# Turning the gated product of eight feed-forwards on VectorE instead of TensorE

## What is computed

```python
D_MODEL, SEQ, D_FF = 1024, 256, 2816

def swiglu(h, w13, w2):                    # feed-forwards 0 to 3
    a, b = jnp.split(h @ w13, 2, axis=-1)
    return (jax.nn.silu(a) * b) @ w2

def _half_ffn(x, g_pre, g_post, w_gate, w_up, w_down):   # feed-forwards 4 to 7
    h = _rmsnorm(x, g_pre)
    f = (jax.nn.silu(h @ w_gate) * (h @ w_up)) @ w_down
    return x + 0.5 * _rmsnorm(f, g_post)

mod = c_act @ ada_w[l] + ada_b[l]          # 9 x 1024 columns for each layer of the first block
sh1, sc1, g1, sh2, sc2, g2, sh3, sc3, g3 = jnp.split(mod, N_ADA, axis=-1)
```

## Time and profile before

| | |
|---|---|
| median of 3 runs | 2158.02 us (2157.7 to 2168.08) |
| span of the profiled execution | 2156.2 us |
| TensorE busy | 2100.3 us |
| VectorE busy | 1474.4 us |
| ScalarE busy | 1002.2 us |
| mean granted TensorE clock | 0.995 |
| transposes of the gated product (L793) | 352 matmuls |
| ScalarE's copy of it (L1615), 80 of them to g_hi | 577 ns |
| VectorE's low part of it (L2332), 80 of them to g_lo | 683 ns |

### The profile page before, as it was taken

How to read it: one execution, slowest core, us unless ns; L and a number is a source line. 1 busy time by engine, 2 the same in 40 slices (tenths; PEclk the granted TensorE clock), 3 DMA queues, 4 the chain that set the end, 5 groups by cost and what they waited for, 6 DMA issues and landing times.

```text
span 2156.2 us, 31249 instructions
## 1 busy us (share of the span) xinstructions
PE 2100.3 (97%) x12249; PEld 1832.9 (85%) x12249; DVE 1474.4 (68%) x2058; ACT 1002.2 (46%) x1415; POOL 31.1 (1%) x33
## 2 busy tenths in 40 slices
PE   7999999999999999999999999999999999989998
PEld 5888998888888988888888888888887888988887
DVE  7988878888888646674465558975457546677444
ACT  3434555334443555443364446464446445555443
POOL 0000000000000000000000000010000000001000
PEclk9999999999999999999999999999999999999999
DMA  8888446886787441275555542235554554425552
GB/s 343 302 309 306 164 174 227 318 307 239 295 298 264 152 142 46 74 275 191 177 168 182 194 176 104 73 102 211 184 186 164 187 190 143 155 79 178 193 181 92
DMA packets 75606, 417.46 MB, mean 194 GB/s; under 512 B 5888, under 2 KB 6016, under 8 KB 51840
## 3 DMA queue, kind: packets, MB, share of 16 engines
q1 hardware_dynamic: 75520, 416.27, 53.9%
HBM read 415.20 MB, written 1.05 MB: 193 GB/s over the span
## 4 chain that ended last, share of the span: by engine, by line
PE 88%; DVE 7%; ACT 2%; DMA 1%; issue 1%; SPq 0%; DVEq 0%; ACTq 0%
PE AB L750 13%; PE AB L752 13%; PE AB L751 13%; PE Y L293 9%; PE Y L295 9%; PE Y L294 9%; PE AB L293 2%; PE AB L295 2%; PE AB L294 2%; PE Y L1377 2%; DVE lo L2074 2%; PE N L793 2%; PE M L693 1%; PE Y L750 1%; PE Y L751 1%; PE Y L752 1%
## 5 line engine op out<-in xcount | busy, mean ns | idle before, releaser
L2074 DVE TENSOR_TENSOR lo<-raw,hi 128x2048 fp32r<-128x2048 f32 x310 | 708.3, 2287 | 384.3 <-ACT hi L1527 383.8
L1527 ACT ACTIVATE hi<-raw 128x2048 fp32r<-128x2048 f32 x322 | 615.0, 1913 | 539.5 <-PE Y L295 254.7
L750 PE MATMUL AB<-hi,h_hi 128*128 128x512 f32 x1280 | 506.4, 396 | 1.5 <-DVE lo L2074 1.5
L752 PE MATMUL AB<-hi,h_lo 128*128 128x512 f32 x1280 | 499.3, 390 | 0.0
L751 PE MATMUL AB<-lo,h_hi 128*128 128x512 f32 x1280 | 498.3, 389 | 0.0
L752 PEld LDWEIGHTS AB<-hi,h_lo 128*128 128x128 f32 x1280 | 240.3, 188 | 51.3
L750 PEld LDWEIGHTS AB<-hi,h_hi 128*128 128x128 f32 x1280 | 240.4, 188 | 49.2 <-DVE lo L2074 1.7
L751 PEld LDWEIGHTS AB<-lo,h_hi 128*128 128x128 f32 x1280 | 240.7, 188 | 47.9
L293 PE MATMUL Y<-g_hi,hi 128*128 128x256 f32 x664 | 188.2, 283 | 0.0
L294 PE MATMUL Y<-g_lo,hi 128*128 128x256 f32 x664 | 187.9, 283 | 0.0
L295 PE MATMUL Y<-g_hi,lo 128*128 128x256 f32 x664 | 187.8, 283 | 0.0
(11 more groups left out here) (437 smaller groups left out, 3223.2 us busy)
## 6 DMA issues: line engine op xcount, KB each, us to landing
raw<-slabs SPq DMA_DIRECT2D x322, 1024.0 KB, 5.0
ada_raw<-ada SPq DMA_DIRECT2D x34, 2048.0 KB, 8.1
ada_raw<-ada SPq DMA_DIRECT2D x2, 1024.0 KB, 14.8
kT<-ada SPq DMA_DIRECT2D x1, 1024.0 KB, 10.3
vt<-ada SPq DMA_DIRECT2D x1, 1024.0 KB, 12.3
x<-x_t SPq DMA_DIRECT2D x1, 1024.0 KB, 14.3
out_t<-x SPq DMA_DIRECT2D x4, 256.0 KB, 3.0
vec<-vectors SPq DMA_DIRECT2D x1, 462.0 KB, 3.1
```

Of the source, the lines that this page charges most:

```text
L750: nc.tensor.matmul(out_, h_hi[:, k, at], w_hi, start=start, stop=False)
L752: return nc.tensor.matmul(out_, h_lo[:, k, at], w_hi, start=False, stop=stop)
L1527: nc.scalar.activation(hi[slot][:, :], raw[slot][:, :], ACT.Copy).then_inc(hi_done[slot], 1)
L2074: nc.vector.tensor_tensor(lo[slot][:, :], raw[slot][:, :], hi[slot][:, :].bitcast(F32), ALU.subtract).then_inc(lo_done[slot], 1)
```

## The change

LAY_FROM is 0, so every condition `f < LAY_FROM` is false, and all eight feed-forwards change. In steps 1 to 10 TensorE no longer turns the gated product; at the end of steps 1 to 9 it only waits for `gf_done`. VectorE, between the split of the second up slab and the split of the down slab, runs `lay_gated`: sixteen block transposes, each of 32 partitions and 4 blocks of 32 columns, from `gf` into `silu`, with the signal `g_laid` on the last. ScalarE's `g_split` and VectorE's `gate_lo` read `silu` instead of N. Since `silu` now holds the turned product until `gate_lo` has read it, ScalarE's next silu waits for `glo_done` as well. The eleventh product of each feed-forward still goes through TensorE and N.

```diff
--- before.py
+++ after.py
@@ -253,6 +253,7 @@
         h_half = sem("h_half")
         acc_ready = sem("acc_ready")
         g_turned = sem("g_turned")
+        g_laid = sem("g_laid")
         ot_ready = sem("ot_ready")
         maps_ready = sem("maps_ready")
         head_var = sem("head_var")
@@ -463,6 +464,8 @@
             return [((j + r) % 3, (j + r) // 3 - 1) for r in range(3)]
 
         DEFERRED = (6, 8, 9, 10, 11)
+
+        LAY_FROM = 0
 
         def pre_gain(n):
             l, j = divmod(n - 6, 3)
@@ -901,7 +904,7 @@
                 def step(i, ada, first=False, last=False):
                     pe.wait_ge(lo_done[ring[0][0]], i + (ring[0][1] + 1))
                     up(ring[0][0], 0)
-                    if first:
+                    if first and f < LAY_FROM:
                         turn_gated(i + g0)
                     pe.wait_ge(lo_done[ring[1][0]], i + (ring[1][1] + 1))
                     up(ring[1][0], 1)
@@ -911,7 +914,10 @@
                     def behind():
                         if ada:
                             cols(i + (q0 - 1))
-                        turn_gated(i + (g0 + 1))
+                        if f < LAY_FROM or last:
+                            turn_gated(i + (g0 + 1))
+                        else:
+                            pe.wait_ge(gf_done, i + (g0 + 1))
 
                     down(ring[2][0], first=first, between=behind if last else None)
                     if not last:
@@ -1610,9 +1616,18 @@
                     else:
                         nc.scalar.activation(h_hi[:, k, :], hf[:, k, :], ACT.Copy).then_inc(hh_ready, 1)
 
-            def g_split(g, to=g_hi):
-                act.wait_ge(g_turned, g + 1)
-                nc.scalar.activation(to[:, :], N[:, :], ACT.Copy).then_inc(ghi_done, 1)
+            def g_split(g, f):
+
+                if f < LAY_FROM:
+                    act.wait_ge(g_turned, g + 1)
+                else:
+                    act.wait_ge(g_laid, g - (LAY_FROM * NSTEP + f - LAY_FROM) + 1)
+                nc.scalar.activation(g_hi[:, :], N[:, :] if f < LAY_FROM else silu[:, :], ACT.Copy).then_inc(ghi_done, 1)
+
+            def last_g_split(f):
+
+                act.wait_ge(g_turned, (f + 1) * NSTEP if f < LAY_FROM else LAY_FROM * NSTEP + f - LAY_FROM + 1)
+                nc.scalar.activation(z_hi[:, :], N[:, :], ACT.Copy).then_inc(ghi_done, 1)
 
             def ffn(f):
                 g0 = c.take("g", NSTEP)
@@ -1622,9 +1637,11 @@
                 j0 = c.take("slab", 3 * NSTEP - 4) - 1
                 (sa, na), (sb_, nb), (sw, nw) = step_slots(j0)
 
-                def silu_of(a, slot, n):
+                def silu_of(a, slot, n, g=None):
 
                     act.wait_ge(used[slot], n)
+                    if f >= LAY_FROM and g is not None:
+                        act.wait_ge(glo_done, g)
                     if f >= 4:
                         for t in range(TT):
                             ins = nc.scalar.activation(silu[:, t * T:(t + 1) * T], a[:, t], ACT.Silu,
@@ -1638,11 +1655,11 @@
                     if first and f >= 4:
                         split(sb_, i + nb)
                         act.wait_ge(root_ready, TT * c["stat"] + TT)
-                    silu_of(a_, slot_b, n_b)
+                    silu_of(a_, slot_b, n_b, None if first else i + (g0 - 1))
                     if not (first and f >= 4):
                         split(sb_, i + nb)
                     split(sw, i + nw)
-                    g_split(i + (g0 - 1))
+                    g_split(i + (g0 - 1), f)
                     if a:
                         split(sa, i + (na + 1))
 
@@ -1654,11 +1671,11 @@
                 step(NSTEP - 1, ab_tok[:, :, A], sb_, NSTEP - 1 + nb, a=False)
                 j = c["slab"] - 2
                 next_slab()
-                silu_of(ab_tok[:, :, A], j % 3, j // 3 + 1)
+                silu_of(ab_tok[:, :, A], j % 3, j // 3 + 1, g0 + NSTEP - 1)
                 n_ahead = min(2, NSLAB - c["slab"])
                 if n_ahead:
                     next_slab()
-                g_split(g0 + NSTEP - 1, z_hi)
+                last_g_split(f)
                 if f >= 4:
                     c.take("stat")
                 sqrt_table()
@@ -2327,9 +2344,19 @@
                                                          ALU.mult)
                 ins.then_inc(gf_done, 1)
 
-            def gate_lo(g, to_hi=g_hi, to_lo=g_lo):
+            def lay_gated(g):
+
+                dve.wait_ge(gf_done, g + 1)
+                src = gf[:, :].rearrange("p (t c n) -> p c t n", t=TT, c=2)
+                to = silu[:, :].rearrange("p (c t n) -> p c t n", c=2, t=TT)
+                for a in range(0, P, 32):
+                    for b in range(0, P, 32):
+                        ins = nc.vector.transpose(to[b:b + 32, :, :, a:a + 32], src[a:a + 32, :, :, b:b + 32])
+                ins.then_inc(g_laid, 1)
+
+            def gate_lo(g, src, to_hi=g_hi, to_lo=g_lo):
                 dve.wait_ge(ghi_done, g + 1)
-                nc.vector.tensor_tensor(to_lo[:, :], N[:, :], to_hi[:, :].bitcast(F32), ALU.subtract
+                nc.vector.tensor_tensor(to_lo[:, :], src[:, :], to_hi[:, :].bitcast(F32), ALU.subtract
                                         ).then_inc(glo_done, 1)
 
             def ffn(f):
@@ -2355,8 +2382,10 @@
                     gated(i + (g0 - 1), b)
                     if not (first and f >= 4):
                         split(sb_, i + nb)
+                    if f >= LAY_FROM:
+                        lay_gated(i + (g0 - 1))
                     split(sw, i + nw)
-                    gate_lo(i + (g0 - 1))
+                    gate_lo(i + (g0 - 1), N if f < LAY_FROM else silu)
                     if out_:
                         mod_out(i + (q0 - 2))
                     if mac_:
@@ -2374,7 +2403,7 @@
                 gated(g0 + NSTEP - 1, ab_tok[:, :, B])
                 if c["slab"] < NSLAB:
                     split(c["slab"] % 3, c["slab"] // 3)
-                gate_lo(g0 + NSTEP - 1, z_hi, z_lo)
+                gate_lo(g0 + NSTEP - 1, N, z_hi, z_lo)
                 if n_ada == NSTEP - 1:
                     c["last_mod"] = q0 + NSTEP - 2
                 if n_ada:
```

## The result

The changed kernel takes 2254.41 us (median of 4 runs, 2251.56 to 2255.12), the kernel before 2157.86 us beside it: ratio 1.0433, 95% interval 1.0416 to 1.045. That is 96.5 us slower. The span of the profiled execution is 2252.7 us against 2156.2, so its difference is 96.5 us as well.

The account below looks back on a forecast made before the run. TensorE bounds the kernel; VectorE would bound steps with modulation work. Feed-forwards 0 and 1 add 74.2 us, 2 adds 27.4, 3 adds 4.9, 4 to 7 give back 8.8: 97.7, plus 13.6 for the clock, 2269.3 us; range 2200 to 2310.

Parts of the forecast that it names:

- The bound moves to VectorE in loaded steps: In steps with modulation work, VectorE would need 20.65 us where TensorE needs 16.98, so TensorE waits for the gate product.
- loaded steps: The 30 of 80 steps that carry modulation work on VectorE, in feed-forwards 0 to 3; 17.34 us long before the change.
- The price of the block: VectorE's sixteen transposes per step: 0.31 us each plus 0.02 us between, 5.3 us together, called L.
- 34 places: Where the block's length was taken to be on the path: 20 + 8 + 2 + 4 over the feed-forwards.
- Priced as L2409 overlaps, 3.7 us: Rival: VectorE's transposes overlap as independent full-width operations do, block 3.7 us, kernel 2208 us; chance 0.17.
- pieces on different quarters run side by side: Rival: VectorE's sixteen transposes cost what four full-width ones do, 1.24 us, fitting into the idle; kernel 2122 us; chance 0.04.
- The law, 34 L - 82.5: Time added to the whole kernel in us, before the clock, for a VectorE block of L us; 97.7 us forecast.
- The crossing of 2.4 us a block: The VectorE block length per step at which gain and loss cancel, 0.15 us per piece.
- What the removal gives: Four TensorE transposes fewer per step, 0.45 us each group; at most 36 us over all 80.
- light steps: The 50 of 80 steps without modulation work; VectorE has room, and steps were to shrink from 16.81 to 16.36 us.
- The first step of feed-forwards 4 to 7: TensorE would wait 2.3 us for the low part, less 0.45 for the removed turn: +1.8 us each.
- The clock: TensorE's granted clock falls after its waits, costing 1.7 us once per feed-forward, 13.6 us in all.

Follow-up runs that it names:

- e6: The changed kernel with one in-place transpose of 128 partitions x 512 elements instead of sixteen, so the product is not the true one: 2129.28 us, ratio 0.9844.
- e4: The changed kernel with each of the sixteen transposes writing to the partitions it reads, so no block moves between quarters: 2201.34 us, ratio 1.0189.
- e5: The changed kernel with only the eight transposes that read the lower 64 partitions, half of the product left unturned: 2166.15 us, ratio 1.0037.
- e9: The changed kernel with the block's two loops swapped: the quarter written stays for four transposes, the quarter read changes at each; 2253.51 us, ratio 1.0449.
- e2: The changed kernel with only pieces 1 to 9 of feed-forwards 4 to 7 turned on VectorE, the rest on TensorE as before: 2141.22 us, ratio 0.9908.
- e1: The changed kernel with only feed-forwards 4 to 7 turning on VectorE, 0 to 3 as before the change: 2154.1 us, ratio 0.9962.
- e7: The changed kernel with TensorE's wait in loaded steps filled by zero matmuls into the free bank N, same results computed: 2252.28 us, ratio 1.0421.

## Why the prediction was right

I forecast 2269.3 us in a range of 2200 to 2310; it came to 2254.4. Of the 111.3 us, 96.5 came.

- **The bound moves to VectorE in loaded steps.** Right, by the full VectorE in feed-forward 0, by the step of 20.34 us (20.65 forecast), and by e6, where the same path with a short block is faster than before. Step less block is 15.27 us in the changed kernel and in e4, and 15.26 in e5: only the block changes VectorE's step.
- **The price of the block.** 5.3 us forecast, 5.07 measured: 0.303 us a transpose (0.31) and 0.014 us between (0.02). Times 34 places this is 7.8 us of the miss. Both halves of the estimate came from operations of another kind: the duration from a transposing reduction with its length scaled down, the distance from four additions of 4 elements that change quarters. Neither was luck. The step from 512 elements to 128 costs (705 - 303) / 384 = 1.05 ns an element between e6's transpose and these, as the subtraction assumed (1.044). And e4 and e9 show that the distance was right for its reason. Priced as L2409 overlaps, 3.7 us, the block would have been about e4's 3.60 us, and the forecast 46 us too low (2208 us). That pieces on different quarters run side by side is refuted: each starts after the one before has ended.
- **The law, 34 L - 82.5.** With the measured 5.07 us it gives 89.9 us, and the eight feed-forwards measured 91.8, of which 1.6 are the clock in feed-forward 6. It also carried e5 and e4 within 3 us. The crossing of 2.4 us a block fits e5: at 2.54 us the kernel is 0.4% slower than before. It doesn't reach down to e6 (0.71 us), where loaded steps are TensorE's again.
- **What the removal gives.** 0.45 us forecast, 0.48 measured in feed-forwards 4 to 7 (16.80 to 16.32) and 0.44 in 2 and 3 (17.10 to 16.66). The sum over light steps was therefore slightly low.
- **The first step of feed-forwards 4 to 7.** A wait of 2.3 us was forecast ahead of the down product. The timeline of TensorE, feed-forward 4 (answering):

```profile
1236.83 0.47 PE L294 MATMUL Y<-hi,g_hi 128*128 128x512 f32 x1 [2.24 <-DVE g_lo L2359]
```

  e2 removes it by leaving piece 0 on TensorE, and gains 2.0 us per feed-forward over e1.
- **The clock.** This is the term that was mis-sized: 13.6 us forecast, as one exposed fall of 3.4 us, worth 1.7, for each feed-forward. The falls came (mean clock 0.978), and inside loaded steps they are hidden, as e7 shows. Exposed were 6.0 us between feed-forwards 0 and 1 (3.9) and 1 and 2 (2.1), and one fall in feed-forward 6, about 1.6 us. At the ends of 0 and 1 the fall is there as forecast, but lasts 6.8 us; the rest of the 3.9 fits a further fall of 3.4 us in the mixer behind feed-forward 0, at 358.9. The kernel before and e7 have none there, but whether the edit brings it is not shown. Feed-forwards 2 and 3 took the path back without a visible fall, and in 4, 5 and 7 the wait of 2.2 us brought none. With the 1.5 us that the kernel before loses between 4 and 5 and the changed one doesn't, the clock made 6.1 instead of 13.6 us, which is 7.5 us of the miss.

TensorE's timeline where feed-forward 0 ends (answering), then slices of 2 us behind feed-forward 0, in the mixer, and behind feed-forward 1 (stretch, length, TensorE busy, clock, DMA share, GB/s):

```profile
255.04 0.49 PE L639 MATMUL M<-ada_lane,over_quads 128*128 128x128 f32 x2 [3.17 <-DVE ada_lane L2134]
257.93 1.11 PE L796 MATMUL N<-ident,gf 128*128 128x128 f32 x4 [2.40 <-DVE gf L2336]
...
258.00:260.00 2.00, 2.00 (x10) 0.50 0.83 250
260.00:262.00 2.00, 2.00 (x11) 0.50 0.98 414
...
360.00:362.00 2.00, 2.00 (x12) 0.50 0.00 0
...
602.00:604.00 2.00, 2.00 (x11) 0.50 1.03 340
```

Price and clock together, 7.8 + 7.5 = 15.3 us, are the whole difference of 14.8 us and half a microsecond more. The mechanism and its place were right. What the forecast had too high is the price of a transpose, by little, and the clock, which it charged in eight places and which showed in three.

## What to carry to other kernels

An engine that is busy 68% of the span can be full in the stretch where new work lands: read the idle of one loop step, 1.99 us here, not the share of the page. The loss is then (block - idle) for each step, whatever is taken off the other engine in those steps; the gain exists only in the steps with room, and the same edit placed there alone turned 96 us of loss into 24 us of gain. Price small operations by the distance between starts of operations that switch partitions as the new ones do, since an overlap read off full-width ones would have made the block 1.4 us too short.

## What the runs showed of the hardware

- A transpose of 32 partitions x 128 float32 elements lasts 303 ns when the quarter read or written changes at each, and 0.26 us in most cases where both stay (e4); one of 128 x 512 lasts 705 ns (e6). The distance between starts is 0.21 us with unchanged quarters (e4), and 0.316 us when the quarter read (e9) or the quarter written (the changed kernel) changes at each.
- A wait's length alone doesn't tell whether the granted clock falls. After 2.24 us of idle ahead of 1236.83 it stayed at 1.00 (2.4 GHz), and after 1.92 us ahead of 1753.97 it fell. In most loaded steps the falls came in every second step: after a wait of 2.88 us the step ran slower, so that the next wait was 1.55 us, and no fall followed. Timeline rows, then slices of 2 us (TensorE busy, clock, DMA share, GB/s), changed kernel:

```profile
177.06 0.49 PE L753 MATMUL AB<-hi,h_hi 128*128 128x512 f32 x1 [2.88 <-DVE gf L2336]
197.35 0.49 PE L753 MATMUL AB<-hi,h_hi 128*128 128x512 f32 x1 [1.55 <-DVE gf L2336]
...
178.00:180.00 2.00, 2.00 (x7) 0.50 0.93 397
180.00:182.00 2.00, 2.00 (x8) 0.64 0.99 408
...
198.00:200.00 2.00, 2.00 (x11) 1.00 0.94 403
...
1238.00:1240.00 2.00, 2.00 (x10) 1.00 0.95 397
```
